# Expert weights in 8 MB transfers, by pieces at the ends, with the overflow list spread over one expert

## The chip, the core and the metric

The kernel runs on one core of a Trainium2 chip. The metric is device time in microseconds for one execution. TensorE (PE) multiplies matrices, VectorE (DVE), ScalarE (ACT) and GpSimd (POOL) work on elements, SyncE (SP) issues the transfers from device memory (HBM), and 16 DMA engines carry them.

## The reference

One layer of a hybrid decoder over 256 tokens of width 1024, in float32: a Mamba-2 mixer, a cross-attention into 256 memory rows, and a mixture of 32 experts of which each token takes 4. The last part matters here:

```python
def moe_ffn(h, w_router, b_router, w_gate_up, b_gate_up, w_down, b_down):
    logits = (ht @ w_router) + b_router
    top_logits, top_idx = lax.top_k(logits, TOP_K)            # 4 of 32
    gates = jax.nn.softmax(top_logits, axis=-1)
    ...
    gu = xb @ w_gate_up[e] + b_gate_up[e]                     # 1024 x 2048, 8 MB an expert
    gate = jnp.minimum(gu[..., :D_FF], 7.0)
    up = jnp.clip(gu[..., D_FF:], -7.0, 7.0)
    act = (up + 1.0) * (gate * jax.nn.sigmoid(gate * 1.702))
    return act @ w_down[e] + b_down[e]                        # 1024 x 1024, 4 MB an expert
    ...
    out = zeros.at[row_tok].add(ys * row_gate)                # weighted sum over a token's experts
```

Every sub-layer starts with an RMS norm and ends with a residual add; a final RMS norm follows.

## The kernel before

The first 320 us or so are the mixer and the cross-attention; then come the router and the 32 experts, one after the other. An expert has 64 slots for tokens (`SLOTS`). For each pair of experts TensorE gathers the tokens with a one-hot matrix (`gather_half`, L951). For expert c it then runs, in `regular` (L1063): the transposes of the scatter weights (L964), `gate_up` of c (L971), for odd c a half of the gather for the next pair, `down` of c-1 (L1003), the transposes of c's gate and up (L993), `scatter` of c-1 into four accumulating banks (L1017), and for odd c the gather's other half. ACT and DVE copy results out of PSUM and compute the gated activation (`swiglu`, L1866) beside it. The first two experts are written out, then a loop runs over pairs 1 to 7, then `biases_and_list` (L1077), then a loop over pairs 8 to 14, then `last_experts` (L1041).

The weights of all experts, 403 MB, are read once. There are three places for them in SBUF: gate-up of even experts and of odd ones, 8 MB each, cut in four pieces (`GP`), and w_down, 4 MB, in two (`DP`). `w_gate_up` is laid out so that a partition holds `GR` neighbouring rows: with `GR` = 4 a transfer of half an expert (4 MB, `load_gate_up_group`, L389) puts 32 KB in one piece into each partition, and one of a quarter (`load_gate_up`, L374) 16 KB. `GS` is the number of pieces in such a group, `GJ` the number of groups in an expert. A transfer of w_down (2 MB) has 16 KB per partition.

SyncE issues all of them on one queue, in the order of its program (L488 to L511): gate-up of expert c+2 once `gate_up` of expert c has used the pieces (`gu_used`), then w_down of c once `down` of c-1 has used them (`dn_used`). For the last experts the order turns over: from expert 26 w_down of c goes ahead of gate-up of c+2, with expert 27's gate-up half before and half after w_down(25). Expert 3 and expert 31 go by quarters (`reload_pieces`), the others by halves. w_down of experts 30 and 31 goes into the gate-up slots at the very end (L506). TensorE waits for a group at its first piece (`g_ready`, L978), and for w_down by pieces (`d_ready`, L1008).

Experts with more than 64 tokens are listed in `biases_and_list` and worked off in an extra loop, if there are any. That block also adds the down biases, weighted by `gate`: `gate` is transposed, copied by ACT into `scatT`, and multiplied with `b_down` in eight matmuls; then come counts, places and the list, with DVE's `overflow_list` (L1910) between, and a register load of the number of extra experts.

Ahead of the first expert the norm of the second 128 tokens (`norm_apply(3, 1, ...)`, L1827) stands in DVE's program between the top-4 mask and the ranks; it reads h and the gains with a stride of `GR` elements. TensorE's `first_gather` waits for it (`normed`) and for the one-hot (`hot_ok`).

Of the kernel before, what the change touches and what calls it, by code (L numbers as in the profile page):

```python
# [33 lines left out]
P = 128  # L34
# [22 lines left out]
GR = 4  # L57
# [3 lines left out]
MIDDLE = 8  # L61
HSLOTS = 4
# [3 lines left out]
def build(nc, x, mem, mixer_norm, xattn_norm, mem_norm, ffn_norm, w_in, conv_w, conv_b, dt_bias, a_log,  # L66
          d_skip, ssd_norm, w_out, xa_w_q, xa_w_kv, xa_w_o, w_router, b_router, w_gate_up, b_gate_up,
          w_down, b_down, final_norm, out):
    with ExitStack() as ctx:
# [99 lines left out]
        wdt = part(wdt_f, 0, KD * HEADS, r="p (k h) -> p k h", k=KD)  # L169
        lrow = nc.alloc_sbuf_tensor_at("lrow", [P, TC, P], F32R, offset=wdt_at)  # L170
# [82 lines left out]
        wq_ok = sem("wq_ok")  # L253
        sums_ok, extra_ps = sem("sums_ok"), sem("extra_ps")
# [137 lines left out]
        def g_loads(n, c):  # L392


            extra = (0 if n == GP + 1 else 1) if n >= GP else 0 if c < 2 else 1 if n else 2
            if n % GS == 0:
                return c // 2 + 1 + extra
            return min(c // 2, 1) + 1 + extra + (1 if n >= GP and c >= NE - 1 else 0)
# [9 lines left out]
        def _(sp):  # L408
# [61 lines left out]
            def reload_pieces(e):  # L470

                for s in range(GP):
                    sp.wait_ge(gu_used, GP * (e - 2) + s + 1)
                    load_gate_up(sp, e, e % 2, s)
# [55 lines left out]
        def _(pool):  # L530
# [29 lines left out]
            for c in range(TC):  # L560
                nc.gpsimd.tensor_tensor(rall[:, c, :, :], by8[:, :].unsqueeze(2).to_broadcast([P, HPG, P]),
                                        acx[:, c, :].unsqueeze(1).to_broadcast([P, HPG, P]),
                                        ALU.mult).then_inc(rall_ok, 1)


        @block.tensor
        def _(pe):
# [373 lines left out]
            def first_gather(half, ms):  # L941

                for m in ms:
                    k = 4 * (m % 2) + 2 * (m // 2) + half
# [6 lines left out]
            def gather_half(i, pair, half):  # L951
# [5 lines left out]
                for m in range(4):  # L957
                    k = 4 * (m % 2) + 2 * (m // 2) + half
# [12 lines left out]
            def gate_up(i, c, expert, first=False):  # L971


                for s in range(GP):
# [3 lines left out]
                    pe.wait_ge(g_ready[n], 16 * i + 16 * g_loads(n, c) if n % GS == 0 else 16 * g_loads(n, expert))  # L978
# [84 lines left out]
            def regular(i, c, expert, gathers=True):  # L1063

                scatter_transpose(i, c)
                pe.wait_ge(gate_b, 2 * i + c)
                pe.wait_ge(up_b, 2 * i + c)
                gate_up(i, c, expert)
                if gathers:
                    gather_half(i, 1, 0)  # L1070
                down(i, c - 1)
                transposes(i, c)
                scatter(i, c - 1)
                if gathers:
                    gather_half(i, 1, 1)

            def biases_and_list():  # L1077

                pe.wait_ge(gate_ok, 1)
                for t in range(TC):  # L1080
                    last = tr(ps[D_BANK][0:NE, P * t:P * (t + 1)], gate[:, t, :], ident)
                last.then_inc(gT_ps, 1)
                pe.wait_ge(gT_ok, 1)
                pe.wait_ge(ld_bdn, 16)
                for n in range(2):
                    for t in range(TC):
                        mm(ps[4 + 2 * t + n][:, :], scatT[0:NE, P * t:P * (t + 1)],
# [905 lines left out]
```

## Time and profile before

| | |
|---|---|
| median of 3 runs | 1248.57 us |
| their range | 1247.25 to 1249.79 us |
| the profiled execution | 1247.7 us |
| its span, first to last instruction | 1245.9 us |
| TensorE busy, share of the span | 94% |
| DMA queue of the weights, share of 16 engines | 87.7% |
| chain that ended last: TensorE | 53% |
| chain that ended last: DMA | 42% |

The profile is of one execution. The chain is followed back from the last instruction, at each step to what released it. A DMA share of 1.00 means that all 16 engines always had a packet; it can stand a little above that, since neighbouring packets overlap. Times in the rows are from the span's start.

### The profile page before, as it was taken

How to read it: one execution, taken by the hardware profiler on the slowest of the kernel's cores; microseconds unless marked ns; L12 is line 12 of the kernel's file. 1: busy time of each engine (PE TensorE's matmuls, PEld its weight loads, DVE VectorE, ACT ScalarE, POOL GpSimd, SP SyncE). 2: the span in 40 equal slices, each digit the busy share in tenths (PEclk: the TensorE clock that was granted, in tenths of full speed). 3: DMA queues.
4: the chain of work that ended last, by engine and by line, in shares of the span. 5: the costliest groups of instructions: out<-in, count | busy, mean ns of one | idle time of the engine just before them, and what ended most of it. 6: DMA issues, size and time to landing. Idle time of an engine off the chain costs nothing.

```text
span 1245.9 us, 15217 instructions
## 1 busy us (share of the span) xinstructions
PE 1175.0 (94%) x6198; PEld 621.5 (50%) x6198; DVE 391.1 (31%) x703; ACT 275.9 (22%) x421; POOL 7.5 (1%) x27
## 2 busy tenths in 40 slices
PE   9999999999999999998988999899999998999996
PEld 8998887898634433333333333334433333343432
DVE  5987677546312211111111112102211111112112
ACT  5655566345211101011000011001101011011102
POOL 1000000000000000000000000000000000000000
PEclk9999999999999999999999999989999999999999
DMA  9454333469799999999999999999999999999996
GB/s 340 155 203 142 129 135 136 162 262 378 304 407 413 434 426 429 431 431 430 433 433 430 429 436 426 433 417 430 436 426 430 429 431 430 432 423 428 432 424 249
DMA packets 49191, 454.30 MB, mean 365 GB/s; under 512 B 5692, under 2 KB 5860, under 8 KB 30084
## 3 DMA queue, kind: packets, MB, share of 16 engines
q1 hardware_dynamic: 48976, 453.73, 87.7%
q8 instruction: 26, 0.43, 0.1%
q10 hardware_dynamic: 180, 0.07, 0.0%
q14 instruction: 9, 0.07, 0.0%
HBM read 452.74 MB, written 1.05 MB: 364 GB/s over the span
## 4 chain that ended last, share of the span: by engine, by line
PE 53%; DMA 42%; DVE 3%; issue 1%; DVEq 1%; SPq 1%; ACT 0%
DMA ring<-in_moe_w_down 41%; PE ps L985 14%; PE ps L1013 11%; PE ps L647 3%; PE ps L649 3%; PE ps L648 3%; PE ps L1023 2%; PE ps L960 2%; PE ps L662 1%; PE ps L664 1%; PE ps L663 1%; PE ps L779 1%; DMA wring<-in_ssd_w_in 1%; DVE wlo L1504 1%; PE ps L1000 1%
## 5 line engine op out<-in xcount | busy, mean ns | idle before, releaser
L1013 PE MATMUL ps<-ring,wring 128*64 128x512 f32 x960 | 216.5, 597 | 49.3 <-DMA ring<-in_moe_w_down 49.3
L985 PE MATMUL ps<-odd_ring,wring 128*64 128x512 f32 x1024 | 225.5, 598 | 0.9 <-DVE wring L1871 0.8
L985 PE MATMUL ps<-ring,wring 128*64 128x512 f32 x1024 | 223.5, 594 | 0.0
L1136 ACT ACTIVATE wring<-ps 128x512 f32<-128x512 f32 (+2 forms) x101 | 52.4, 535 | 499.8 <-PE ps L985 424.4
L1013 PEld LDWEIGHTS ps<-ring,wring 128*64 128x64 f32 x960 | 65.1, 137 | 188.7 <-issue 112.5
L1863 DVE COPY wring<-ps 128x512 f32<-128x512 f32 x32 | 22.1, 691 | 404.7 <-PE ps L985 404.7
L985 PEld LDWEIGHTS ps<-odd_ring,wring 128*64 128x64 f32 x1024 | 73.7, 138 | 141.6 <-issue 139.6
L985 PEld LDWEIGHTS ps<-ring,wring 128*64 128x64 f32 x1024 | 71.9, 137 | 139.3 <-issue 139.1
L1871 DVE TENSOR_TENSOR wring<-ps,bguT 128x512 f32<-128x512 f32 x64 | 41.2, 685 | 296.7 <-PE ps L1000 296.7
L1136 ACT ACTIVATE ysb<-ps 128x512 f32<-128x512 f32 x36 | 21.4, 596 | 260.6 <-PE ps L1013 246.4
L960 PEld LDWEIGHTS ps<-wring 128*128 128x128 f32 x480 | 55.8, 191 | 23.5 <-issue 23.5
L1023 PE MATMUL ps<-ysb,wring 64*128 64x512 f32 x256 | 63.6, 615 | 0.7 <-ACT ysb L1136 0.7
L960 PE MATMUL ps<-wring 128*128 128x128 f32 x480 | 61.5, 281 | 0.0
L1504 DVE TENSOR_TENSOR wlo<-wring,lo_ring 128x2048 fp32r<-128x2048 f32 x23 | 52.2, 2286 | 11.3 <-ACT lo_ring L1136 11.3
L1136 ACT ACTIVATE lo_ring<-wring 128x2048 fp32r<-128x2048 f32 x24 | 45.4, 1930 | 10.1 <-PE ps L649 5.6
L664 PE MATMUL ps<-hi_ring,wlo 128*128 128x256 f32 x160 | 45.3, 283 | 0.0
L1000 PEld LDWEIGHTS ps<-cst,wring 128*128 128x128 f32 x256 | 27.4, 141 | 26.9 <-issue 25.2
L648 PE MATMUL ps<-wlo,hi_ring 128*128 128x512 f32 x96 | 37.4, 389 | 0.0
L1000 PE MATMUL ps<-cst,wring 128*128 128x128 f32 x256 | 35.0, 280 | 0.9 <-DVE wring L1863 0.9
L1136 ACT ACTIVATE wring<-wring 128x512 f32<-128x512 f32 x32 | 20.2, 630 | 60.7 <-DVE wring L1875 60.7
L1023 PEld LDWEIGHTS ps<-ysb,wring 64*128 64x128 f32 x256 | 22.0, 186 | 22.5 <-issue 20.9
L1538 DVE SCALAR_TENSOR_TENSOR ring<-ps,parT,ring 128x255 f32<-128x255 f32 (+2 forms) x72 | 31.1, 476 | 1.8
(312 smaller groups left out, 1311.6 us busy)
## 6 DMA issues: line engine op xcount, KB each, us to landing
ring<-in_moe_w_down SPq DMA_DIRECT2D x59, 2048.0 KB, 25.3
ring<-in_moe_w_gate_up SPq DMA_DIRECT2D x28, 4096.0 KB, 22.9
odd_ring<-in_moe_w_gate_up SPq DMA_DIRECT2D x26, 4096.0 KB, 24.7
wring<-in_ssd_w_in SPq DMA_DIRECT2D x9, 2048.0 KB, 8.5
odd_ring<-in_moe_w_gate_up SPq DMA_DIRECT2D x9, 2048.0 KB, 15.7
ring<-in_moe_w_down SPq DMA_DIRECT2D x10, 1024.0 KB, 33.8
wring<-in_xa_w_kv SPq DMA_DIRECT2D x4, 2048.0 KB, 8.0
wring<-in_ssd_w_out SPq DMA_DIRECT2D x4, 2048.0 KB, 7.9
```

Of the source, the lines that this page charges most:

```text
L647: mm(ps[bank][:, :], xh[:, k0 + k, tok], wh, start=start and k == 0, stop=False)
L648: mm(ps[bank][:, :], xh[:, k0 + k, tok], wl, start=False, stop=False)
L649: last = mm(ps[bank][:, :], xl[:, k0 + k, tok], wh, start=False, stop=stop and k == KD - 1)
L664: last = mm(dst, wl[:, c0:c0 + P], x_hl[0][:, k, :], start=False, stop=k == KD - 1)
L960: last = mm(ps[G_BANK][:, P * m:P * (m + 1)], xn[:, t, P * k:P * (k + 1)], onehot[:, t, :, :], start=t == 0, stop=t == TC - 1)
L985: last = mm(ps[a][SLOTS * half:SLOTS * (half + 1), :], xs[:, m, c % 2, :], w[:, kk, c0:c0 + 512], start=s + kk == 0, stop=s + kk == GP)
L1000: last = tr(ps[a][:, P * j:P * (j + 1)], gus[:, c0:c0 + P], ident)
L1013: last = mm(ps[D_BANK][SLOTS * half:SLOTS * (half + 1), :], act[:, k, :], w[:, kk, 512 * half:512 * (half + 1)], start=k == 0, stop=k == K ...
L1023: last = mm(ps[4 + 2 * t + half][:, :], rows[r, P * t:P * (t + 1)], ysb[r, :], start=False, stop=True, skip_group_check=True)
L1136: return nc.scalar.activation(out_, in_, func, **kw)
L1504: v.tensor_tensor(lo_, raw_, hi.bitcast(F32), ALU.subtract).then_inc(wl_ok, 1)
L1871: v.tensor_tensor(gu[:, a, :, :, :], ps[a][:, :].rearrange("p (j h s) -> p j h s", j=4, h=2), b4[:, a, :, :].unsqueeze(3).to_broadcast([P, ...
```

## The change

`GR` goes from 4 to 8: a partition holds eight neighbouring rows, one group is a whole expert, and a transfer of 8 MB has 64 KB per partition. Experts named in `BY_PIECES` go by quarters, with 16 KB per partition. `AHEAD` says how many quarters of gate-up(c+2) go ahead of w_down(c): four, from c = 23 three, then two, one and none. The order of SyncE's transfers is written out in one loop instead of a hardware loop with ends.

```diff
-GR = 4
+GR = 8
 GJ = 2 * GP // GR
 GS = GR // 2
+BY_PIECES = (3, 4, 5, 6, 7, 25, 26, 27, 31)
+AHEAD = ((0, 4), (23, 3), (24, 2), (25, 1), (26, 0))
...
-            reload_pieces(3)
-            reload_down(1, 0, 1)
-            reload_gate_up(4, 0, 4)
-            reload_down(2, 0, 2)
-            with sp.Fori(1, PAIRS - 4, 1) as i:
-                for c in (1, 2):
-                    reload_gate_up(2 * i + (c + 2), i, c + 2)
-                    reload_down(2 * i + c, i, c)
-            reload_gate_up(NE - 5, 0, NE - 5, range(0, GJ // 2))
-            reload_down(NE - 7, 0, NE - 7)
-            reload_gate_up(NE - 5, 0, NE - 5, range(GJ // 2, GJ))
-            for e in range(NE - 6, NE - 3):
-                reload_down(e, 0, e)
-                reload_gate_up(e + 2, 0, e + 2)
-            reload_down(NE - 3, 0, NE - 3)
-            reload_pieces(NE - 1)
+            for c in range(1, NE - 2):
+                e = c + 2
+                ahead = [n for first, n in AHEAD if c >= first][-1]
+                for part_, s0, s1 in ((0, 0, ahead), (1, ahead, GP)):
+                    if part_:
+                        reload_down(c, 0, c)
+                    if e in BY_PIECES:
+                        reload_pieces(e, range(s0, s1))
+                    else:
+                        reload_gate_up(e, 0, e, range(s0 // GS, s1 // GS))
```

The norm of the second 128 tokens goes from DVE to POOL, in two instructions; `rst_ok` is set by DVE's reciprocal:

```diff
+            pool.wait_ge(ld_g, 16)
+            pool.wait_ge(std, 2 * 3 + TC)
+            nc.gpsimd.tensor_tensor(xn[:, 1, :].rearrange("q (k p) -> q k p", k=GR),
+                                    h[:, 1, :].rearrange("q (p k) -> q k p", k=GR),
+                                    g_ffn.rearrange("q (p k) -> q k p", k=GR), ALU.mult)
+            pool.drain()
+            pool.wait_ge(rst_ok, 1)
+            nc.gpsimd.tensor_scalar(xn[:, 1, :], xn[:, 1, :], rst[:, 3, 1:2], None, ALU.mult).then_inc(normed, 1)
...
-            norm_apply(3, 1, xn, h, g_ffn)
-            dve.drain()
```

`biases_and_list` is cut into four parts that stand in the turn of expert 18, and moves from bank 2 to bank 3; the transposed `gate` has a place of its own, `gateT`. DVE's part is cut in two, before and after `swiglu`:

```diff
+            def regular(i, c, expert, gathers=True, lists=False):
                 scatter_transpose(i, c)
+                if lists:
+                    turn_gate()
                 pe.wait_ge(gate_b, 2 * i + c)
                 pe.wait_ge(up_b, 2 * i + c)
                 gate_up(i, c, expert)
+                if lists:
+                    biases_and_counts()
                 if gathers:
                     gather_half(i, 1, 0)
                 down(i, c - 1)
+                if lists:
+                    places()
                 transposes(i, c)
                 scatter(i, c - 1)
+                if lists:
+                    overflow_list()
                 if gathers:
                     gather_half(i, 1, 1)
...
-            regular(0, 1, 1)
-            regular(0, 2, 2, False)
-            with pe.Fori(1, MIDDLE, 1) as i:
+            for i in range(0, 4):
+                regular(i, 1, 2 * i + 1)
+                regular(i, 2, 2 * i + 2, False)
+            with pe.Fori(4, MIDDLE, 1) as i:
...
-            biases_and_list()
+            regular(MIDDLE, 1, 2 * MIDDLE + 1)
+            regular(MIDDLE, 2, 2 * MIDDLE + 2, False, True)
+            pe.wait_ge(lst_ok, 1)
             extra = pe.value_load(lst_i[0:1, 32:33], min_val=0, max_val=MAX_EXTRA)
-            with pe.Fori(MIDDLE, PAIRS - 1, 1) as i:
+            with pe.Fori(MIDDLE + 1, 12, 1) as i:
...
+            for i in range(12, PAIRS - 1):
+                regular(i, 1, 2 * i + 1)
+                regular(i, 2, 2 * i + 2, False)
```

The gathers' order of columns (`k` in `first_gather` and `gather_half`) and the counts of `g_ready` follow the new layout. ACT and DVE get the same turn for pair 8 written out.

## Rows read from the trace of the kernel before

**Rows 1.** The page's part 2: rate of transfer in 40 equal slices of the span
```profile
GB/s 340 155 203 142 129 135 136 162 262 378 304 407 413 434 426 429 431 431 430 433 433 430 429 436 426 433 417 430 436 426 430 429 431 430 432 423 428 432 424 249
```

**Rows 2.** Chain that ended last, in order of time: start us, us, what
```profile
454.14 25.34 DMA ring<-in_moe_w_down
...
483.35 25.35 DMA ring<-in_moe_w_down
...
800.89 3.65 PE ps L1013 x16
...
918.22 3.68 PE ps L1013 x16
```

**Rows 3.** SyncE's timeline: start us, us from first to last issue, line, count
```profile
464.51 7.15 SPq L390 DMA_DIRECT2D odd_ring<-in_moe_w_gate_up  x2
...
495.53 7.18 SPq L390 DMA_DIRECT2D ring<-in_moe_w_gate_up  x2
```

**Rows 4.** Queue in 508.5 to 525.1 us: packets, MB, share of 16 engines
```profile
q1 hardware_dynamic: 235, 7.18, 100.4%
```

**Rows 5.** The same in 498.6 to 505.6 us
```profile
q1 hardware_dynamic: 198, 2.98, 100.0%
```

**Rows 6.** The page's part 6: issue, count, KB each, us to landing
```profile
out<-hs SPq DMA_DIRECT2D x4, 256.0 KB, 2.4
```

**Rows 7.** Timeline, 312 to 342 us: start, us, engine, line, operation
```profile
322.74 2.13 DVE L1488 SCALAR_TENSOR_TENSOR wring<-hs,rst 128x1024 f32<-128x1024 f32 x1
...
322.74 0.29 ACT L1136 ACTIVATE nrm<-nrm 128x1 f32<-128x1 f32 x1
...
326.83 2.05 DVE L1488 SCALAR_TENSOR_TENSOR wring<-hs,rst 128x1024 f32<-128x1024 f32 x1
...
329.80 4.54 PE L946 MATMUL ps<-wring 128*128 128x128 f32 x24 [1.04 <-DVE wring L1834]
```

**Rows 8.** POOL's timeline, DVE's timeline, and the page's part 5 (last row)
```profile
122.28 3.75 POOL L561 TENSOR_TENSOR lo_ring<-by,rank 128x1024 fp32r<-128x1024 f32 x2 [116.81 <-PE ps L649]
...
125.00 3.18 DVE L1504 TENSOR_TENSOR wlo<-wring,uth 128x2048 fp32r<-128x2048 f32 x1
...
L1504 DVE TENSOR_TENSOR wlo<-wring,lo_ring 128x2048 fp32r<-128x2048 f32 x23 | 52.2, 2286 | 11.3 <-ACT lo_ring L1136 11.3
```

**Rows 9.** TensorE's and DVE's timeline; last row: busy by stretch, then PEclk
```profile
808.27 4.21 PE L1087 MATMUL ps<-wring 32*128 32x512 f32 x8 [0.46 <-ACT wring L1136]
...
812.41 1.01 PE L1091 MATMUL ps<-cst,mask 128*128 128x1 f32 x4
...
816.81 0.68 PE L968 MATMUL ps<-cst,wring 128*128 128x128 f32 x2 [1.63 <-issue]
...
817.42 15.99 PE L985 MATMUL ps<-odd_ring,wring 128*64 128x512 f32 x64
...
749.85 0.69 DVE L1882 TENSOR_TENSOR wring<-wring 128x512 f32<-128x512 f32 x1
...
812.00:814.00 2.00, 1.75 (x7) 1.25 (x6) 0.16 (x1) 0.00 (x0) 0.00 (x0) 0.50 0.87 377
```

**Rows 10.** Instruction fetches in the queues, 440 to 460 and 820 to 860 us
```profile
q8 instruction: 1, 0.02, 0.3%
...
q8 instruction: 2, 0.03, 0.3%
```

**Rows 11.** Chain, SyncE's timeline, landing of those two issues, waits of TensorE
```profile
1125.19 13.88 PE ps L985 x64
...
1177.28 13.91 PE ps L985 x64
...
1146.36 0.91 SPq L390 DMA_DIRECT2D ring<-in_moe_w_gate_up  x2
...
ring<-in_moe_w_gate_up SPq DMA_DIRECT2D x2, 4096.0 KB, 29.7
...
PE ps L1036 <- DMA ring<-in_moe_w_down: 1.9, 4, 0.6
```

More of the change, by code:

```diff
@@ L390, in load_gate_up_group, with transfers, g_loads @@
             sp.dma_start(gu_group(odd, j), gu_rows[e, j, :, :, :]).then_inc(g_ready[GP * odd + GS * j], 16)
[L392 to L398, printed above, removed]
+        def transfers(n, e):
+            if e % 2 != n // GP:
+                return 0
+            if e == 1:
+                return 1 if n == GP + 1 else 2
+            if e == 2:
+                return 2 if n else 3
+            return 1 if e == 0 or e in BY_PIECES or n % GS == 0 else 0
+        def g_loads(n, e):
+            return sum(transfers(n, x) for x in range(e + 1))
         def d_loads(s, c):
@@ L468, in _, with reload_pieces @@
             sp.dma_start(bdn[0:NE, :], b_down).then_inc(ld_bdn, 16)
-            def reload_pieces(e):
-                for s in range(GP):
+            def reload_pieces(e, pieces_):
+                for s in pieces_:
                     sp.wait_ge(gu_used, GP * (e - 2) + s + 1)
@@ L977, in gate_up @@
                     n = GP * (c % 2) + s
-                    pe.wait_ge(g_ready[n], 16 * i + 16 * g_loads(n, c) if n % GS == 0 else 16 * g_loads(n, expert))
+                    pe.wait_ge(g_ready[n], 16 * i + 16 * (g_loads(n, expert) - (expert - c) // 2) if n % GS == 0 else
+                               16 * g_loads(n, expert))
                     w = gu_w(n)
@@ L1061, in last_experts, with turn_gate, biases_and_counts @@
                 scatter(i, 1, scatT_last).then_inc(fin_ps, 1)
[L1063 to L1077, printed above, removed]
+            def turn_gate():
                 pe.wait_ge(gate_ok, 1)
+                pe.wait_ge(xsb_ok, MIDDLE + 2)
                 for t in range(TC):
-                    last = tr(ps[D_BANK][0:NE, P * t:P * (t + 1)], gate[:, t, :], ident)
+                    last = tr(ps[G_BANK][0:NE, P * t:P * (t + 1)], gate[:, t, :], ident)
                 last.then_inc(gT_ps, 1)
+            def biases_and_counts():
                 pe.wait_ge(gT_ok, 1)
@@ L1414, in _, with regular @@
             sigmoid(0, 0)
-            def regular(i, c, gathers=True):
+            def regular(i, c, gathers=True, lists=False):
                 scatter_out(i, c)
+                if lists:
+                    act_.wait_ge(gT_ps, 1)
+                    fn(gateT[0:NE, :], ps[3][0:NE, 0:SEQ], ACT.Copy).then_inc(gT_ok, 1)
                 gate_out(i, c)
@@ L1429, in _ @@
                 regular(i, 2, False)
[L1430 to L1431 removed]
+            regular(MIDDLE, 1)
+            regular(MIDDLE, 2, False, True)
             act_.wait_ge(lst_ok, 1)
             extra = act_.value_load(lst_i[0:1, 32:33], min_val=0, max_val=MAX_EXTRA)
[L1434 removed]
+            with act_.Fori(MIDDLE + 1, PAIRS - 1, 1) as i:
                 regular(i, 1)
@@ L1897, in _, with regular @@
             swiglu(0, 0, 0)
-            def regular(i, c, gathers=True, out=act):
+            def regular(i, c, gathers=True, out=act, lists=False):
                 if gathers:
```

65 lines of the change are left out of this document (41 added, 24 removed).

## The prediction

> **What bounds the kernel now.** I read the page's row of transfer rate by slices first [rows 1], then the chain of waits in order of time [rows 2], then SyncE's issues [rows 3]. From slice 13 on (about 405 us) the rate stands at some 430 GB/s to the end: the reader is to see a plateau, not peaks. The chain names the same thing: TensorE's second half of down waits for the last w_down piece, and the landings of that piece are 508.70 - 479.48 = 29.22 us apart [rows 2]. One expert is 12.58 MB; 12.58 MB in 29.22 us is 430.6 GB/s. The packets explain the period without a remainder. In a stretch that holds only 32 KB packets, 7.18 MB are 219 of them, so 1.004 x 16.6 us x 16 / 219 = 1217.6 ns each [rows 4]. In a stretch of 16 KB packets, 182 of them give 1.000 x 7.0 x 16 / 182 = 615.4 ns [rows 5]. Gate-up is 16 packets of 32 KB per DMA engine and down 16 of 16 KB: 19.48 + 9.85 = 29.33 us. So from about 340 us the engines are never without work, and only three things can move the end: when the plateau begins, a hole in it, or work after the last landing. TensorE needs (1177.28 - 1125.19) / 2 = 26.0 us for an expert where it does not wait [rows 11] and has slack, except before 427 us, after the overflow list and from 1064 us to the end, where the chain runs through it.
>
> **Packets of 64 KB.** What a packet costs beyond its bytes is 2 x 615.4 - 1217.6 = 13 ns. Twenty experts (8 to 24, 28 to 30) go from 16 packets per engine to 8: 20 x 8 x 13 ns = 2.1 us less. Seven experts (4 to 7, 25 to 27) go from 16 packets of 32 KB to 32 of 16 KB: 7 x 16 x 13 ns = 1.5 us more; 3 and 31 went by pieces before. Sum -0.6 us. No row has a 64 KB packet. Bounds: nothing saved, if a 64 KB row is cut in two (+1.5), and twice the 13 ns on the saved packets (-2.7); I take the 13 ns, since the nearest rows differ by it.
>
> **The later free and the later landing of 8 MB.** A group of 8 MB waits for all of gate_up(c), where the first 4 MB went after half of it. In the steady state the second half's issue is over at 495.53 + 7.18 = 502.71 [rows 3], 23.2 us after the landing at 479.5; in a turn without gathers at 471.66, 21.4 us after the landing at 450.3. The queue is empty 29.2 us after the landing, less the part of a DMA that is start and finish: the 256 KB stores take 2.4 us, 0.6 of it bytes, so 1.8 [rows 6]. That leaves 29.2 - 1.8 - 23.2 = 4.2 us, and 6.0 without gathers. No hole: 0. Behind the waiting issue on SyncE stands w_down, which waits for a later TensorE instruction anyway. TensorE's wait for the whole 8 MB costs nothing there, because w_down of the expert before lands after it in the queue. Pieces for experts 4 to 7 let expert 4's load start at the first quarter of gate_up(2) instead of at half. The slice of 374 to 405 us stands at 413 instead of 430 GB/s [rows 1], so at most 4% of 31 us, 1.3 us, is to be had. I take 0 (bounds -1.3 and 0): the row is a mean of 16 engines, part of it is 16 KB packets, and a load lands with its last engine.
>
> **The overflow list.** Before, it stands alone on TensorE between two experts, and yet costs little: from 800.89 to 918.22 are 117.33 us for four landings, 0.5 more than 4 x 29.22 [rows 2]; the half-expert issue had kept the queue full. After, set the landing of w_down(17) at 0. gate_up(18) ends at 23.2 - 29.2 = -6.0; turning gate adds about 0.6 (bound: the 0.68 of two transposes [rows 9]); biases 4.21 and counts 1.01 [rows 9] bring -0.2. Then both halves of down follow, 2 x 3.65 [rows 2], to 7.1, and the matmul of places to 7.4. swiglu ends 4.4 us after a down (749.85 + 0.69 = 750.5 against 742.5 + 3.65, the landing nine turns after 479.5 [rows 2, 9]): 11.8. DVE's list and the register load take the 1.63 us and the next transposes the 0.68 of rows 9: 14.1. gate_up(19) takes 13.9 at full clock [rows 11], so its free comes at 28.0, where 29.2 - 1.8 = 27.4 was the limit: a hole of 0.6 us against 0.5 lost before, +0.1. At the 15.99 us that gate_up took behind the list in this trace [rows 9], the hole is 2.7: +2.2. Lower bound -0.5. I take +0.1, because after this change full-rate matmuls stand between the narrow ones; the other end is a rival.
>
> **The norm on POOL.** It leaves DVE (326.83, 2.05 us [rows 7]). The rank of the tokens waits 1.0 us for it, so at best first_gather starts at 328.75 instead of 329.80 [rows 7]: -1.05. POOL may start when ACT's second root is done, 323.03 [rows 7]. Its nearest row is 1.9 us for a 128x1024 product [rows 8], and DVE's strided one takes 2.1 where a contiguous one of that size takes about 1.2 (half of 2286 ns [rows 8]), so two POOL instructions are 3.8 to 6 us, 327 to 330. In rows 8 a DVE product of two SBUF operands takes 3.18 instead of 2.29 us exactly while POOL still runs. DVE's masked and one-hot products have two SBUF operands too, so they queue behind POOL and POOL behind DVE's first norm (to 324.87). I take first_gather at 329.5, -0.3; bounds -1.05 and +0.9. SyncE's wait for `normed` moves with it, to about the same 329. The Trainium skill, "SBUF — State Buffer", section "Who interferes with whom", says that DVE and GpSimd share a port pair as an exclusive lock; by that rule, which the stretched product bears out, the term is -0.3, and without it -1.05. DVE's remaining norm with a stride of 8 instead of 4: 0, it already takes the strided time.
>
> **Straight code.** TensorE's loop for experts 3 to 8, 17, 18 and 25 to 30 is written out: 14 experts more. A loop's body of two experts took two fetches of 16 KB [rows 10], so some 14 more, 14 x 0.615 / 16 = 0.5 us of the queue if they spread, and 14 x 0.6 if all met the engine that lands last. One at 449 us left the spacing at 29.2 [rows 2, 10], and two around 840 us fell in the stage that lost 0.5 [rows 2, 10], so at most 14 x 0.25 = 3.5. I take 0.5.
>
> **The end.** Bringing w_down forward by a quarter at experts 25 to 27 moves no bytes past the end; TensorE gets ahead earlier, which is then lost at gate_up(28): 0. But with w_down ahead, gate_up(30) follows its own load closely. Its second 4 MB land at about 1181.2: the two groups were issued from 1146.36 on (at 1146.6 in the mean) and landed 29.7 us later in the mean [rows 11], that is at 1176.3, and the second half of 9.74 us (4 MB at 430.6 GB/s) after that. gate_up(30) began at 1177.28 [rows 11], on the first half. Waiting for 8 MB it begins at 1181.2: +3.9. At the end TensorE had 1.9 us of waits for DMA left [rows 11]: +2.0. Bounds 0.8 and 2.5 (how far the last landing sets the end).
>
> **Sum.** -0.6 + 0 + 0.1 - 0.3 + 0.5 + 2.0 = +1.7 us. The profiled execution took 1247.7 us (span 1245.9), so 1249.4 for such a one; it lies 0.9 under the median of 1248.57. On the median: 1250.3, +0.14%.
>
> **Rivals.** (A) Slower: the clock falls behind the spread list. In the trace it stood at 0.50, the 1.2 GHz level, 4 us after the biases had begun, and gate_up behind the list was slowed by 2.1 us [rows 9]. If it does so again during biases and down, gate_up(19) ends 2.1 us later, or about 4 with down slowed too: 1252.4 to 1254.3. For it: the same narrow matmuls and a 3 us stop before gate_up(19); against: they are cut by full stages. It decides once free comes past 27.4. (B) Faster: the large packets save the double, POOL is quick, the spread list leaves no hole and TensorE is not late at the end: -2.7 - 1.05 - 0.5 + 0.5 = -3.75, 1244.8. Against it: the landing of expert 30's gate-up is fixed by the bytes ahead of it. (C) Slower by much: an 8 MB transfer starts more than 4.2 us after its wait; each us beyond is lost in 17 experts, so one is +17, 1267. Against: the 2.4 us of rows 6. (D) The change doesn't do what it says: 64 KB rows are cut to 32 KB, nothing is saved: 1252.4. (E) The end costs nothing but all else holds: 1248.3. The Trainium skill, "DMA: Bandwidth & Descriptors", section "Anatomy of one DMA — SWDGE (gpsimd) path", gives about 2 us of fixed cost per DMA; twenty transfers fewer would be 40 us, some 1210 us. Packets already fill 29.33 of 29.22 us, so the trace does not bear it out and it is left 1 in 100, out of B's share.
>
> **How the numbers follow.** Forecast 0.45 (own range 1248.8 to 1251.8), A 0.18, B 0.18, D 0.08, E 0.07, C 0.04. A measurement of this kernel tells about 0.2% (2.5 us) from no change: 1246.1 to 1251.1. Faster is B, 0.18. Same is E and the forecast without its upper 0.06: 0.46. Slower is that 0.06 with A, D and C: 0.36. The range 1244.5 to 1254.0 leaves out C and the fringes of A and B.
>
> **What would show it.** Mean time of a 64 KB packet 2422 ns, and landings of w_down 29.1 us apart for experts 9 to 22; 2435 ns or 32 KB packets speak for D. The rate row without a dip near 887 us, or with one of 1 to 3 us, together with the granted clock there (A). POOL's two instructions ending by 329, first_gather at 329.5. gate_up(28), (29) and (30) waiting for DMA, gate_up(30) beginning near 1182, and no waits for DMA in the last downs. I am wrong if gate_up(30) begins by 1178, if a hole stands in every turn, or if the last bytes land over 3 us from 1231 us.

## The result, and the profile after

The changed kernel takes 1255.8 us (median of 6 runs, 1253.7 to 1257.7); the kernel before, in the same rounds, 1246.4 (1245.0 to 1249.8). The ratio is 1.0074 with a 95% interval of 1.0064 to 1.0084: slower by about 9.2 us. Forecast was 1250.3 with a range to 1254.0, so the side that was given 36% came, and by more than the range allowed.

The page of the changed kernel, parts 1 to 3: span; POOL; granted clock, share of the DMA engines and rate in 40 slices; instruction fetches.

```profile
span 1254.5 us, 14824 instructions
...
PE 1178.3 (94%) x6198; PEld 628.4 (50%) x6198; DVE 392.3 (31%) x702; ACT 276.0 (22%) x421; POOL 15.7 (1%) x29
...
PEclk9999999999999999999999999998999999999999
DMA  9454333469799999999999999999899999999995
GB/s 342 150 202 142 128 134 135 171 264 377 281 405 429 427 426 429 430 433 435 441 432 428 433 433 428 433 431 424 368 433 412 430 429 427 427 432 430 431 423 230
...
q8 instruction: 41, 0.67, 0.2%
```

The span is 8.6 us longer (1245.9 before). Against [rows 1] the plateau is the same but for one slice: 368 GB/s at 878 to 909 us, and in the slice ahead of it the granted clock has its one 8. Ahead of the plateau, the slice of 314 to 345 us carries 281 instead of 304 GB/s.

The chain of waits of the changed kernel, in order of time (start us, us, what): half of w_down for experts 15 and 16, for 19 and 20, then gate_up(28) and gate_up(30).

```profile
803.73 3.68 PE ps L1027 x16
...
832.88 3.65 PE ps L1027 x16
...
925.55 3.68 PE ps L1027 x16
...
954.70 3.68 PE ps L1027 x16
...
1130.47 15.65 PE ps L999 x64
...
1188.74 13.95 PE ps L999 x64
```

Set beside [rows 2] this is a ledger. At expert 15 the changed kernel is 803.73 - 800.89 = 2.8 us late, at expert 19 925.55 - 918.22 = 7.3 us, at the end 8.6. In the steady state it gains: landings are 832.88 - 803.73 = 29.15 us apart where 29.22 were before. From 16 to 19 there are 92.67 us for three landings, 5.2 more than 3 x 29.15. So about 3 us are lost before expert 15, 5 behind the overflow list and 1 at the end. By the completion records of w_down, 1.9 of the first 2.8 us stood at expert 7; two steps at experts 8 and 9 added 1.3 (see the straight code below), and closer landings gave back 0.4 up to expert 15. The same matmul ahead of the changed stretch already began 0.8 us later in this execution (L902 at 320.76, L889 before at 319.95).

### The profile page after: what moved, and what is told of

The parts are those of the page before. It is cut to its first block, busy times and chain, and to the rows that moved or that the text cites. A ratio compares the mean times of both kernels' runs of the same rounds, so it can differ in the third digit from the quotient of the medians.

```text
span 1254.5 us, 14824 instructions
## 1 busy us (share of the span) xinstructions
PE 1178.3 (94%) x6198; PEld 628.4 (50%) x6198; DVE 392.3 (31%) x702; ACT 276.0 (22%) x421; POOL 15.7 (1%) x29
## 4 chain that ended last, share of the span: by engine, by line
PE 53%; DMA 41%; DVE 3%; DVEq 1%; issue 1%; ACT 0%; SPq 0%
DMA ring<-in_moe_w_down 34%; PE ps L999 15%; PE ps L1027 11%; DMA ring<-in_moe_w_gate_up 6%; PE ps L660 3%; PE ps L662 3%; PE ps L661 3%; PE ps L1037 2%; PE ps L973 1%; PE ps L675 1%; PE ps L677 1%; PE ps L676 1%; DMA wring<-in_ssd_w_in 1%; PE ps L1050 1%; PE ps L792 1%; PE ps L1014 1%
## 5 line engine op out<-in xcount | busy, mean ns | idle before, releaser
L1027 PE MATMUL ps<-ring,wring 128*64 128x512 f32 x960 | 219.3, 604 | 45.1 <-DMA ring<-in_moe_w_down 45.1
L999 PE MATMUL ps<-ring,wring 128*64 128x512 f32 x1024 | 225.2, 597 | 5.5 <-DMA ring<-in_moe_w_gate_up 5.5
L1174 ACT ACTIVATE wring<-ps 128x512 f32<-128x512 f32 (+1 forms) x100 | 52.1, 537 | 504.1 <-PE ps L999 435.7
L1027 PEld LDWEIGHTS ps<-ring,wring 128*64 128x64 f32 x960 | 68.1, 138 | 183.6 <-issue 124.2
L999 PEld LDWEIGHTS ps<-ring,wring 128*64 128x64 f32 x1024 | 74.3, 138 | 144.4 <-issue 144.2
L1545 DVE TENSOR_TENSOR wlo<-wring,lo_ring 128x2048 fp32r<-128x2048 f32 x23 | 52.2, 2286 | 11.3 <-ACT lo_ring L1174 11.3
```

What stands on the lines that cost most here:

```text
L999: last = mm(ps[a][SLOTS * half:SLOTS * (half + 1), :], xs[:, m, c % 2, :], w[:, kk, c0:c0 + 512], start=s + kk == 0, stop=s + kk == GP)
L1027: last = mm(ps[D_BANK][SLOTS * half:SLOTS * (half + 1), :], act[:, k, :], w[:, kk, 512 * half:512 * (half + 1)], start=k == 0, stop=k == K ...
L1174: return nc.scalar.activation(out_, in_, func, **kw)
L1545: v.tensor_tensor(lo_, raw_, hi.bitcast(F32), ALU.subtract).then_inc(wl_ok, 1)
```

## The experiments

Twelve kernels ran, each timed against the kernel before. Where an edit is an undoing, the rest of the change stays. In per cent over the kernel before, with the interval; differences between runs are taken from these ratios, since the kernel before was timed anew beside each group of runs:

| run | what it is | median us | over before |
|---|---|---|---|
| (the change) | | 1255.8 | 0.74 (0.64 to 0.84) |
| e1_order | w_down(19) ahead of gate-up(21) | 1262.3 | 1.32 (1.12 to 1.52) |
| e2_norm | norm back on DVE | 1252.3 | 0.57 (0.37 to 0.78) |
| e3_end | experts 28 to 30 by pieces | 1253.8 | 0.59 (0.41 to 0.76) |
| e4_halves | 4 MB transfers again | 1255.6 | 0.70 (0.53 to 0.87) |
| f1_loops | e2, and 4 to 7 by 8 MB, in the loop | 1256.9 | 1.00 (0.82 to 1.19) |
| f2_load | e2, register load later | 1251.2 | 0.40 (0.26 to 0.54) |
| f3_all | f1, f2 and e3 | 1252.5 | 0.61 (0.47 to 0.75) |
| f4_pool | before, norm on POOL | 1249.7 | 0.29 (0.20 to 0.38) |
| g1_rest | e2, f2 and e3 | 1249.7 | 0.28 (0.18 to 0.39) |
| g2_straight | before, straight code | 1249.2 | 0.30 (0.20 to 0.40) |
| g3_two | g1, pieces for 3 and 4 only | 1247.6 | 0.21 (0.11 to 0.31) |
| g4_loops | g1 in loops, pieces for 3 to 6 | 1246.7 | 0.05 (-0.04 to 0.14) |

### The norm on POOL: two runs

Undone in the changed kernel:

```diff
-            pool.wait_ge(std, 2 * 3 + TC)
-            nc.gpsimd.tensor_tensor(xn[:, 1, :]...
-            nc.gpsimd.tensor_scalar(xn[:, 1, :], ...
...
+            norm_apply(3, 1, xn, h, g_ffn)
```

> The changed kernel with the norm of the second half of the tokens back on DVE, as one instruction behind the mask. Theory 1 (POOL delays the first gate_up by about 1.7 us, but by expert 7 only about 1.1 us of that is left in the landings): the first gate_up begins near 334.5 instead of 336.9 us and the time falls by 0.5 to 1.7 us, from 1255.8 to about 1254.7. Rival (what is lost before the queue is full is carried to the end in full): the time falls by 2 to 2.5 us. Third reading (the late start is absorbed wholly): no change, within 0.3 us.

Done alone in the kernel before (the same lines, with GR = 4):

> The kernel before with only the norm of the second half of the tokens moved to POOL, as in the change. Theory 1 (POOL's strided product takes over 5 us and holds DVE's small instructions meanwhile, TensorE stands still for 3.5 us and the clock falls behind it, and what is lost here is carried to the end): DVE's instruction on two numbers per partition takes about 2.6 us instead of 0.17, first_gather begins 3 us later, and the time rises by 2.5 to 4 us, to about 1249.8. Rival (a late first gate_up is absorbed by loads that are not the bound yet): first_gather begins later, but the time rises by less than 1 us.

Measured: e2_norm 0.57% against 0.74, 2.1 us less and so nearest to the rival (what is lost early is carried to the end), but with intervals that overlap; f4_pool 0.29%, 3.6 us (2.5 to 4.7). The price is read from f4_pool: theory 1. In its profile the landings of w_down stand 2.75 us behind those of the kernel before from expert 4 to expert 16, and 2.9 to 3.1 from expert 17 on: lost once, and carried to the end. Those of e2_norm stand 3.2 to 3.5 us ahead of the changed kernel's up to expert 18. The timeline of the changed kernel shows how it comes about (start us, us, engine, line, operation):

```profile
323.98 5.36 POOL L571 TENSOR_TENSOR wring<-hs 128x1024 f32<-128x1024 f32 x1 [197.11 <-ACT nrm L1174]
...
326.73 2.63 DVE L1861 TENSOR_SCALAR gsum<-mx 128x2 f32<-128x2 f32 x1
...
329.52 2.85 POOL L576 TENSOR_SCALAR wring<-wring,rst 128x1024 f32<-128x1024 f32 x1 [0.18 <-issue]
...
329.95 0.76 DVE L1867 TENSOR_TENSOR mask<-rank,lg 128x64 f32<-128x64 f32 x1
...
330.77 0.41 PE L946 MATMUL ps<-mask,cst 128*128 128x32 f32 x2 [3.54 <-DVE mask L1867]
...
331.96 0.43 DVE L1873 TENSOR_TENSOR wring<-iota,rank 128x256 f32<-128x256 f32 x1
...
332.90 3.99 PE L959 MATMUL ps<-wring 128*128 128x128 f32 x24
```

The same stretch of e2_norm:

```profile
326.44 0.17 DVE L1853 TENSOR_SCALAR gsum<-mx 128x2 f32<-128x2 f32 x1
...
327.20 0.23 DVE L1859 TENSOR_TENSOR mask<-rank,lg 128x64 f32<-128x64 f32 x1
...
330.34 2.92 PE L951 MATMUL ps<-wring 128*128 128x128 f32 x24 [1.06 <-DVE wring L1867]
```

DVE's instruction on two numbers per partition ends at 329.36, 0.02 us after POOL's product (323.98 + 5.36 = 329.34). In f4_pool it is the same: POOL ends at 328.74, DVE at 328.76. So DVE was held for as long as POOL's product ran, and with it mask, rank, one-hot and the first gather. POOL's own end was as late: its second instruction ended at 329.52 + 2.85 = 332.37, the one-hot at 332.39, and the gathers wait for both. TensorE stood still for 3.54 us, and behind that the granted clock was 0.50 from 332 to 334 us, the 1.2 GHz level; the 24 gathers took 3.99 us, in e2_norm 2.92 at full clock. From DVE's small instruction to the first gate_up (336.82, and 333.19 in e2_norm) it is 10.1 us with POOL and 6.75 without. The kernel before stood between them with 8.3, since its first gather took 4.54 us [rows 7]. Its clock fell there too (0.51 from 330 to 332 us) without such a stop, and in g3_two the gathers took the same 4.54 us with the norm on DVE; the other kernels without POOL took 2.92. So the lower clock here is not the norm's doing alone.

What bounds is the queue, and the queue waits for POOL's own end: SyncE's next load of weights stands behind `normed`. SyncE's waits (us in total, times, longest us) in the changed kernel, then in e2_norm:

```profile
SPq L388 <- POOL wring L576: 6.5, 1, 6.5
```

```profile
SPq L388 <- DVE wring L1521: 3.8, 1, 3.8
```

The kernel before waits 3.8 us as well, f4_pool 6.7. From 329 to 333 us the queue of the changed kernel moves nothing. Summed over the packets of each trace, the 16 engines stand idle for 5.9 to 6.2 us in this hole in all five kernels with the norm on POOL, and for 3.1 to 3.3 in the nine without: 2.8 us. That is most of the price, and in f4_pool the hole behind it, where the queue waits for TensorE, adds 0.4 over the kernel before. No run takes the two waits apart, the one for POOL's end and the one behind DVE.

The Trainium skill, "SBUF — State Buffer", section "Who interferes with whom", names `tensor_scalar` among the DVE operations that can take the shared port pair, and says that whoever comes second blocks fully and does not merely slow down. The runs agree: 2.63 us for a `tensor_scalar` that takes 0.17.

### Straight code

In the kernel before, TensorE's loops are written out as far as the change writes them out:

```diff
-            with pe.Fori(1, MIDDLE, 1) as i:
+            for i in range(1, 4):
                 regular(i, 1, 3)
                 regular(i, 2, 4, False)
+            with pe.Fori(4, MIDDLE, 1) as i:
...
```

> The kernel before with one thing changed: TensorE's loop is written out for experts 3 to 8, 17, 18 and 25 to 30, as in the change; the instructions that run are the same. Theory 1 (an instruction fetch of 16 KB takes its turn on one DMA engine, and where it meets the engine that lands last it delays every later landing; in the changed kernel two fetches at 589 and 617 us moved the landings by 1.4 us): some 14 more fetches, a larger spread between the first and the last engine, and the time rises by 0.5 to 2 us. Rival (the fetches lie in gaps or spread over the engines, and the 1.4 us came of something else): within 0.4 us of the kernel before.

Measured: 0.30%, 3.7 us (2.5 to 5.0): theory 1, and more than it expected. The instructions are the same, yet the landings move. The chain of g2_straight:

```profile
455.40 25.34 DMA ring<-in_moe_w_down
...
484.62 25.33 DMA ring<-in_moe_w_down
...
802.20 3.65 PE ps L1013 x16
...
920.61 3.68 PE ps L1013 x16
```

The queues of g2_straight from 423 to 427 us, then from 827 to 829 (packets, MB, share of 16 engines):

```profile
q8 instruction: 1, 0.02, 1.5%
...
q8 instruction: 1, 0.02, 3.2%
```

Against [rows 2] g2_straight is 1.26 us late at 455 us, 1.27 at 484, 1.31 at 802 and 2.39 at 921. Up to there it loses in two steps, one before 455 and one between 802 and 921. In between there were six more fetches, up to 616 us, which moved nothing. One fetch of 16 KB took 3.2% of 16 x 2 us, 1.0 us of one engine. The completion records of the trace show that the last of the 16 engines finishes a w_down piece 2.8 us after the first until 418 us and 4.3 us after it from 427 us on, with the fetch of 424 us between, and the second step lies at the fetch of 827 us. The reading is that a fetch delays all that follows when it meets the engine that is already last, and elsewhere costs nothing; the trace doesn't name the engines, but in all profiles each step of over 0.35 us in the landings between 405 and 1200 us that is no hole has a fetch just ahead of it (0.4 to 1.6 us; in the changed kernel 0.6 and 0.6, at 589 and 617 us). At a hole in the queue the spread shrinks, in the changed kernel from 3.4 to 1.7 us behind the list.

The number of fetches is not the whole of it. The kernel before has fetches at 424 and 830 us too, where its landings moved by 0 and 0.5 us; of the added fetches, two moved those of g2_straight, at 1103 and 1150 us, together by 1.5. So how much of the 3.7 us comes of added fetches, and how much of the engine that a fetch happens to meet, this execution does not tell.

The Trainium skill, "Runtime: NRT & Kernel Launch", section "Instruction fetch mechanics", says that instructions come in 16 KiB blocks through a DMA queue of the sequencer's own and that unrolling is preferred where possible. The size agrees with the rows; the advice does not hold for this kernel, where the queue of weights is the bound and the same instructions written out cost 0.30%.

### Behind the overflow list: three runs

```diff
-AHEAD = ((0, 4), (23, 3), ...
+AHEAD = ((0, 4), (19, 0), (20, 4), (23, 3), ...
```

> The changed kernel with one thing moved: SyncE issues w_down of expert 19 ahead of gate-up of expert 21, so that 4 MB more stand in the queue while the 8 MB wait for gate_up(19). Theory 1 (the loss behind the overflow list is a hole of 5.2 us in the transfers, because the 8 MB of expert 21 may start only after the late and slow gate_up(19)): no hole near 890 us, gate_up(19) still takes 16.6 us, and the time falls by 4.5 to 5.2 us, from 1255.8 to about 1251. Rival (TensorE itself is late behind the list and stays late, so that a fuller queue does not help): the hole moves or goes, but the time falls by less than 2 us.

It took 1262.3 us, 1.32% against 0.74: worse by 7.2 us, where theory 1 expected 5 less, and the rival up to 2 less. Both were wrong about the order. SyncE's timeline, of e1_order and of the changed kernel:

```profile
896.41 3.76 SPq L384 DMA_DIRECT2D ring<-in_moe_w_down  x2
900.22 0.43 SPq L395 DMA_DIRECT2D odd_ring<-in_moe_w_gate_up  x1
```

```profile
892.69 0.33 SPq L395 DMA_DIRECT2D odd_ring<-in_moe_w_gate_up  x1
898.25 3.76 SPq L384 DMA_DIRECT2D ring<-in_moe_w_down  x2
```

The first is e1_order. w_down has one pair of buffers, so w_down(19) waits for down(18), which itself follows gate_up(19). Moved ahead it was issued at 896.41, with gate-up of expert 21 held behind it on SyncE until 900.22, and the engines stood still for 7.7 us instead of 5.1. The run tells nothing of theory 1's place, but in its profile the landings fall another 3.2 us behind those of the changed kernel at the list and stay there to the end: what the queue misses is not made good later. Why the median lost 7.2 is not shown by this execution, the fastest of four.

```diff
-            pe.wait_ge(lst_ok, 1)
-            extra = pe.value_load(lst_i[0:1, 32:33], ...
             with pe.Fori(MIDDLE + 1, 12, 1) as i:
...
+            pe.wait_ge(lst_ok, 1)
+            extra = pe.value_load(lst_i[0:1, 32:33], ...
             for i in range(12, PAIRS - 1):
```

> The changed kernel with the norm back on DVE, and besides TensorE's wait for the overflow list and its register load (2.67 + 1.1 us in front of gate_up(19)) moved four experts later, to just before expert 25. Without this second step it took 1252.3 us, with a hole of 3.5 us in the transfers at 886 us. Theory 1 (the hole is the late end of gate_up(19), on which the 8 MB of expert 21 wait): gate_up(19) begins about 3 us earlier, the hole shrinks to under 1 us, and the time falls by 2.5 to 3.5 us, to about 1249.3. Rival (the wait only moves to the next thing that is late, the first half of the gathered tokens or the banks of expert 18): gate_up(19) begins less than 1 us earlier and the time falls by less than 1 us.

Measured: 0.40% against 0.57 for e2_norm, 2.1 us less than it, with intervals that overlap. In the profile the mechanism is plain, though smaller than expected: gate_up(19) begins 1.4 us earlier, not 3. TensorE's timeline, first of the changed kernel, then of f2_load, gate_up(19) with the transposes ahead of it:

```profile
875.42 0.69 PE L981 MATMUL ps<-cst,wring 128*128 128x128 f32 x2 [2.67 <-issue]
876.03 16.61 PE L999 MATMUL ps<-odd_ring,wring 128*64 128x512 f32 x64
```

```profile
874.67 0.44 PE L973 MATMUL ps<-cst,wring 128*128 128x128 f32 x2
875.04 13.95 PE L991 MATMUL ps<-odd_ring,wring 128*64 128x512 f32 x64
```

In f2_load the 2.67 us of standing still are gone, and from the beginning of gate_up(18) to that of gate_up(19) it takes 32.1 us instead of 33.5, though there down(17) was even slower (9.66 us). Three landings from expert 16 on take 88.6 us (833.28 to 921.89), where e2_norm took 91.4 (829.54 to 920.95): 2.8 us of the hole are gone, theory 1. Of these, 1.1 are gate_up(19) at full clock, 13.95 us and not 15.1 as in e2_norm.

```diff
-GR = 8
+GR = 4
...
-                    k = 4 * half + 2 * (m % 2) + m // 2
+                    k = 4 * (m % 2) + 2 * (m // 2) + half
```

> The changed kernel with gate-up again in transfers of 4 MB with 32 KB per partition; pieces, spread list, order of the queue, norm on POOL and straight code stay. Theory 1 (the hole behind the list comes of the 8 MB, which wait for all of gate_up(19), and not of the spread list itself): the hole near 890 us shrinks to under 1 us (-4.5), the end gains 0.8 to 1.0, the smaller packets lose 0.07 us an expert (+1.2): about 1251.4. Rival (the spread list and its slow gate_up(19) cost the time whatever the size of the transfer): the hole stays above 3 us and the time within 2 us of 1255.8.

Measured: 1255.6 us, as the rival says, but the hole is gone, as theory 1 says. Busy time by stretch, then granted clock, DMA share, GB/s; e4_halves and the changed kernel:

```profile
880.00:890.00 10.00, 10.00 (x48) 3.34 (x48) 1.19 (x6) 0.38 (x1) 0.00 (x0) 1.00 0.96 406
890.00:900.00 10.00, 10.00 (x56) 4.43 (x54) 0.69 (x1) 1.19 (x2) 0.00 (x0) 1.00 1.03 444
```

```profile
880.00:890.00 10.00, 10.00 (x46) 3.23 (x44) 0.00 (x0) 0.00 (x0) 0.00 (x0) 0.93 0.84 357
890.00:900.00 10.00, 10.00 (x56) 4.39 (x54) 0.69 (x1) 1.20 (x2) 0.00 (x0) 1.00 0.79 318
```

In its profiled execution e4_halves was behind the changed kernel by 4.4 us before the list (w_down(16) at 837.32 instead of 832.88), of which 1.1 us stood already at the router's first matmuls. So the list and the 8 MB together make the hole, but why the median shows nothing of it stays open: smaller packets account for 1.1 us, and the interval is 4 us wide. Two things on record bear on it. The hole of this list code is not always so large: the engines missed 5.2 us in the changed kernel's profile, 3.5 in e2_norm and 2.1 in e3_end. And without a hole the last engine does not catch up: near the end of e4_halves it finished a piece 6.3 us after the first, in the changed kernel 1.9.

### Pieces for experts 4 to 7

```diff
-BY_PIECES = (3, 4, 5, 6, 7, 25, ...
+BY_PIECES = (3, 25, ...
...
+            with pe.Fori(1, MIDDLE, 1) as i:
+                regular(i, 1, 3)
+                regular(i, 2, 4, False)
```

> The changed kernel with the norm back on DVE, and besides gate-up of experts 4 to 7 in one 8 MB transfer each, so that TensorE's experts 3 to 8 are a loop again. Without this second step it took 1252.3 us; there the landing of w_down lost 0.8 us against the kernel before from expert 1 to 7 and 1.35 us more at experts 8 and 9, where the spread between the first and the last DMA engine grew from 2.6 to 4.1 us. Theory 1 (pieces of 16 KB rows and instruction fetches for straight code cost this): the spread stays near 2.5 us at expert 9 and the time falls by 1.5 to 2.4 us, to about 1250.4. Rival (8 MB transfers at experts 4 to 7 wait for all of gate_up(2) to gate_up(5), while the queue is still short, and leave a hole near 390 us): the time falls by less than 0.5 us or rises.

Measured: 1.00% against 0.57 for e2_norm, 5.4 us more: the rival. Busy time by stretch in f1_loops, then granted clock, DMA share, GB/s, and SyncE's issue of gate-up of expert 4:

```profile
384.00:388.00 4.00, 4.00 (x22) 1.29 (x18) 0.00 (x0) 0.00 (x0) 0.00 (x0) 1.00 0.89 377
388.00:392.00 4.00, 4.00 (x20) 1.29 (x18) 0.00 (x0) 0.00 (x0) 0.00 (x0) 1.00 0.03 12
392.00:396.00 4.00, 4.00 (x22) 1.42 (x20) 0.69 (x1) 0.60 (x1) 0.00 (x0) 1.00 0.77 266
...
393.50 0.33 SPq L395 DMA_DIRECT2D ring<-in_moe_w_gate_up  x1
```

The 8 MB wait until 393.50 for the end of gate_up(2), and the queue runs dry before: the engines miss 6.7 us. In e2_norm the first of four pieces went at 383.04. The pieces are what 8 MB need in the start; of the instruction fetches this run says nothing, since the hole covers them.

### The end

```diff
-BY_PIECES = (3, 4, 5, 6, 7, 25, 26, 27, 31)
+BY_PIECES = (3, 4, 5, 6, 7, 25, 26, 27, 28, 29, 30, 31)
```

> The changed kernel with gate-up of experts 28, 29 and 30 in four pieces of 2 MB instead of 8 MB. Theory 1 (at the end the last landing and TensorE are nearly tied: the last landing comes 7.5 us later than in the kernel before and the end 8.6 us, so TensorE's wait for whole 8 MB is worth 0.8 to 1.0 us, and 3 x 24 more packets per DMA engine at 13 ns take 0.9 us back): gate_up(30) begins several us earlier, the time changes by -1.0 to +0.3 us, about 1255.4. Rival (TensorE's late start of gate_up(30) alone sets the end): the time falls by 2 us or more.

Measured: 0.59% against 0.74, 1.9 us less, with intervals that overlap: nearer to the rival. TensorE's waits for DMA (us in total, times, longest us) in the changed kernel, then in e3_end:

```profile
PE ps L999 <- DMA ring<-in_moe_w_gate_up: 5.5, 2, 4.5
PE ps L999 <- DMA odd_ring<-in_moe_w_gate_up: 3.3, 1, 3.3
```

```profile
PE ps L999 <- DMA odd_ring<-in_moe_w_gate_up: 3.1, 3, 1.3
...
PE ps L1050 <- DMA ring<-in_moe_w_down: 1.8, 4, 0.6
```

The 8.8 us of waits for 8 MB fall to 3.4 (with 0.3 for the even experts, not shown), and the last halves of down wait for their own w_down again, 1.8 us as before [rows 11]: the end is bound by bytes once more. In the changed kernel no last down waits.

### All together

> The changed kernel with four things: the norm back on DVE, experts 4 to 7 in 8 MB transfers with TensorE's loop, TensorE's register load moved to just before expert 25, and gate-up of experts 28 to 30 in pieces. What is left of the change is 64 KB per partition for experts 4 to 24 and the spread list. If the losses are these four and add up (3.5 for the norm, about 2 for straight code and pieces, 3 for the hole, 0.5 to 1 at the end): about 1246, within 0.2% of the kernel before. If 8 MB transfers cost something that none of the four names: 1249 or more.

f3_all took 1252.5 us, 0.61%: more than the four prices allowed, since it carries the hole of f1_loops (6.9 us at 380 to 400). The others' prices follow from the next run, which leaves pieces for 4 to 7 in place.

> The changed kernel with three things: the norm back on DVE, TensorE's register load moved to just before expert 25, and gate-up of experts 28 to 30 in pieces; experts 3 to 7 stay in pieces and in straight code. If the loss of the change is the norm (about 3.5 us), the hole behind the list (2 to 5) and the end (about 0.5), and the hole near 390 us was the whole loss of the run with the loop: no hole at 390 or 886 us, and about 1247.5, within 1.5 us of that; some 1 us over the kernel before is left for straight code and 16 KB packets. Rival (the spread list or 8 MB transfers cost something in the steady state besides): 1250 or more.

g1_rest took 0.28%, between its two theories; with e2, f2 and e3 undone, 0.46% of the 0.74 are gone. What is left is as large as straight code alone. g3_two starts with fewer pieces:

> As the run with the norm back, the register load moved and experts 28 to 30 in pieces, but in the start only experts 3 and 4 by pieces, and TensorE's loop from expert 5 on. If the hole near 390 us came of expert 4's 8 MB alone (they waited for the end of gate_up(2), with only 4 MB of w_down left in the queue): no hole near 420 us, where expert 5's 8 MB wait for the end of gate_up(3); the landings gain 0.4 us by larger packets and up to 1 us by four fetches less, so 0.5 to 1.4 us less than with five experts in pieces, about 1246.5. Rival (the queue is not full enough until expert 7): a hole of 1 to 4 us near 420 us and a time 1 us or more above the run with five.

It took 0.21%: its interval overlaps that of g1_rest, so the difference is not decided. A hole is there, as the rival says, but it did not cost the rival's 1 us: the engines missed about 1.6 us between 400 and 440 us, less than the 6.7 of f1_loops. The last run takes the straight code away, and lets expert 7 come in 8 MB:

```diff
-                    pe.wait_ge(g_ready[n], ... if n % GS == 0 else
+                    pe.wait_ge(g_ready[n], ... if n % GS == 0 or expert in BY_PIECES else
...
+            with pe.Fori(1, 3, 1) as i:
...
-            for i in range(12, PAIRS - 1):
+            with pe.Fori(12, PAIRS - 1, 1) as i:
```

> As the run with the norm back, the register load moved and experts 28 to 30 in pieces (0.28% over the kernel before), with the same transfers but for expert 7, which comes in one of 8 MB; TensorE's code for experts 3 to 6, 7 to 16, 19 to 24 and 25 to 30 stands in four loops of two experts instead of 16 experts written out. Theory 1 (the straight code is most of what was left, as in the kernel before with straight code alone, 0.30%): 8 to 10 instruction fetches fewer and a time 1.5 to 3 us lower, 0 to 0.15% over the kernel before. Rival (what is left is the transfers themselves: 8 MB, 16 KB packets or the order of the queue): no less than 0.25% over it.

Measured: 1246.7 us, 0.05% (-0.04 to 0.14): theory 1. The page of g4_loops and its chain:

```profile
span 1244.0 us, 14900 instructions
...
q8 instruction: 33, 0.54, 0.2%
...
855.88 7.04 PE ps L1019 x32
```

With 64 KB rows, the spread list and the order of the queue kept, and the four costs taken away, the kernel is where it was. down(17) behind the biases takes 7.04 us there, not 8.8.

## Why the prediction was wrong, point by point

**What bounds.** Right in the main. The plateau stood, and most of what was lost lies where it said: before the queue is full, in one hole, and at the end; 1.3 us were lost in the plateau itself. That a load lands with its last engine stands in the prediction, but not what follows for the plateau: one engine's 1 us is everyone's. The last weights landed at 1240.6 us, 7.6 later than before, which its last paragraph named as a sign of being wrong.

**Packets of 64 KB, -0.6.** The mechanism held. The packets of 64 KB were not cut and took 2428 ns in the mean, between the 2422 of the forecast and the 2435 of rival D. Landings came 0.07 us closer together where 8 x 13 ns = 0.10 was expected, some 1.1 us for 15 experts. Summed over all packets of weights from 340 us on, pieces included, an engine worked 851.6 us where it had worked 852.4: -0.8.

**The later free, 0.** No hole in the steady state, as said; rival C did not come. But the margin of 4.2 us was too large: the 8 MB issued at 892.69 landed 23.0 us later, of which 19.5 are bytes at 430.6 GB/s, so start and finish cost 3.5 us here and not the 1.8 read from 256 KB stores [rows 6]. By that the margin was some 2.5, an estimate.

**Pieces for 4 to 7, 0.** Their worth was underrated: without them 8 MB leave a hole of 6.7 us, 5.4 us of time. The sum is not touched, since they were there.

**Overflow list, +0.1.** Here the step failed at two terms, with the path right. gate_up(19) was put at 14.1 us after the landing of w_down(17), which is at 832.83 + 29.14 = 862.0, so at 876.1; it began at 876.0. That is in part luck: biases and counts took 4.3 us where 5.2 were put, down(17) 8.8 where 7.3 were. It then took 16.6 us instead of 13.9, and ended 30.7 us after the landing instead of 28.0. And the limit was 29.2 - 3.5 = 25.7, not 27.4. 30.7 - 25.7 is 5.0; the ledger gives 5.2. The first of the two is rival A, the second nobody's. The clock in the changed kernel (busy by stretch, then granted clock, DMA share, GB/s):

```profile
858.00:860.00 2.00, 2.00 (x5) 0.56 (x4) 0.00 (x0) 0.00 (x0) 0.00 (x0) 1.00 1.01 426
862.00:864.00 2.00, 2.00 (x8) 0.73 (x6) 0.00 (x0) 0.00 (x0) 0.00 (x0) 0.50 0.98 426
872.00:874.00 2.00, 0.75 (x10) 0.18 (x6) 1.85 (x6) 0.63 (x1) 0.00 (x0) 1.00 1.14 492
876.00:878.00 2.00, 2.00 (x7) 0.74 (x8) 0.87 (x4) 0.38 (x1) 0.00 (x0) 0.50 0.85 369
890.00:892.00 2.00, 2.00 (x12) 0.61 (x10) 0.00 (x0) 0.00 (x0) 0.00 (x0) 1.00 0.04 16
```

It stood at 0.50, the 1.2 GHz level, behind the biases, rose, and fell to it again behind 2.7 us in which TensorE stood still. The reason for taking full clock, that full-rate matmuls stand between the narrow ones, was no reason. Six profiles hold the same list code: down(17) was slowed in five of them (8.5 to 8.8 us, in f1_loops 7.1), gate_up(19) in two (16.6 and, in e2_norm, 15.1; 13.95 in the others). So the hole of the changed kernel is not one number; e3_end, with gate_up(19) at full clock, missed some 2 us.

**Norm on POOL, -0.3.** Wrong in sign, and the dearest term beside straight code: +3.6. The step that failed is the end of POOL's work and the wait for it: the two instructions were put at 3.8 to 6 us, ending from 327 to 330, and took 8.2 (5.36 and 2.85), to 332.4; in f4_pool, whose stretch begins when the kernel before's does, to 331.8. The first 1.7 us of the product lie beside DVE's first norm (323.54 + 2.13 = 325.67). SyncE's wait for `normed` was moved "to about the same 329" and given no price, though the queue of weights is the bound: it grew by 2.7 us, and by 2.9 in f4_pool. DVE's products of two operands were expected to queue behind POOL; what was held first was a small one-operand instruction ahead of them, for 2.6 us. The upper bound of +0.9 had been worked out from POOL's durations and TensorE's first gather, without a term for the queue.

**Straight code, +0.5.** The mechanism was named, the size not: 3.7 us (2.5 to 5.0) in the kernel before. The count was right (15 more fetches for 14). A fetch takes 1.0 us of its engine, not 0.6, and in the profile of g2_straight four of them moved the landings. The bound of 3.5 took a mean of 0.25 per fetch; the forecast then sat at its lower end without a row that spoke for it, although [rows 10] showed only three fetches, too few for a rule.

**The end, +2.0.** Right, within its bounds. gate_up(30) began at 1188.74, 11.5 us later than [rows 11], of which some 7.3 are the landings: 4.2 come of waiting for whole transfers, where 3.9 were expected. The end came 1.1 us later than the last bytes did, and undoing it gave 1.9, with intervals that overlap.

**The sum.** By the runs the norm costs 3.6 us, straight code 3.7, the hole 2.1 (f2_load against e2_norm) and the end 1.9: 11.3. Packets give back 0.8 and the list's old place 0.5, which leaves 10.0 where 9.2 were measured; each price has an interval of 1 us or more to either side. The forecast had -0.3, +0.5, +0.1 and +2.0 for these four. So norm and straight code, 7.1 us off together, make up most of the miss, and the hole the rest; that the kernel would be slower was forecast, by 1.7 us.

## What to carry to other kernels

Where a queue of transfers is the bound, price every edit by what it does to that queue's last engine: code written out brings fetches that can land there, and a larger transfer starts later and has a dearer start. Moving an instruction to another engine is priced by everyone who waits for its end, the issuer of the transfers first, and by what is held while it runs, down to the smallest instruction of its neighbour. When a term's bounds are wide, the value between them needs a row of its own; here norm, straight code and list were taken on the kind side of the middle, and all three came out at or above the upper bound.

## What the runs showed of the hardware

A POOL product of 5.4 us held a DVE instruction of two numbers per partition until 0.02 to 0.03 us after its end, in each of five profiles with the norm on POOL. POOL's strided product of 128x1024 took 5.36 to 5.58 us, the first 1.7 us beside a norm on DVE, where its scaling by a number per partition, without a stride, took 2.85. An instruction fetch of 16 KB took 1.0 us of one DMA engine, and the steps in the landings at fetches were 0.4 to 1.6 us. An 8 MB transfer into an idle queue landed 3.5 us later than its bytes account for. The granted clock fell behind the same list code in some executions and not in others.
